# Four operations moved ahead of weight splits, and a tile by tile end, in a two-layer trunk on one core

## The reference, cut to what matters

```python
for l in range(2):
    x = x + 0.5 * swiglu(rmsnorm(x), ffn1_w_in[l], ffn1_w_out[l])       # hidden 2816
    z = rmsnorm(x) @ mix_w_in[l]                                         # 8 parts of 256 columns
    y_a = a_b * conv3(a_c * a_x)
    y_b = u * (tril(W_s) LN(v) + b)
    y_c = silu(LN(conv31(a * sigmoid(g))))
    y_d = scale * grouped_linear(avgpool(w) - w)
    x = x + concat(y_a, y_b, y_c, y_d) @ mix_w_out[l]
    x = x + cross_attention(rmsnorm(x), rmsnorm(mem), wq, wkv, wo)       # 4 heads of 256
    x = x + 0.5 * swiglu(rmsnorm(x), ffn2_w_in[l], ffn2_w_out[l])
return rmsnorm(x, norm_final)
```

## Time and profile before

| | |
|---|---|
| three runs | 1113.24, 1114.97, 1116.08 us (median 1114.97) |
| the profiled execution | 1115.91 us, of which 1113.0 us are the span from first to last instruction |
| PE busy | 1096.5 us (99% of the span), mean granted clock 0.996 |
| DVE, ACT, POOL busy | 710.8, 533.6, 396.1 us |
| read from HBM | 200.79 MB, 181 GB/s over the span |

### The profile page before, as it was taken

The page is one execution under the profiler, slowest core; times in us unless marked ns, Lnnn a source line. Parts: engine busy times, 40 slices in busy tenths (PEclk is TensorE's granted clock), DMA queues, the critical chain, the costliest instruction groups (busy, mean ns, idle before and its releaser), DMA issues.

```text
span 1113.0 us, 13974 instructions
## 1 busy us (share of the span) xinstructions
PE 1096.5 (99%) x5294; PEld 922.4 (83%) x5294; DVE 710.8 (64%) x821; ACT 533.6 (48%) x583; POOL 396.1 (36%) x775
## 2 busy tenths in 40 slices
PE   8999999999999999999999999999999999999996
PEld 6887888889798888888888888888988988888885
DVE  6666556799756656655566665568996557666552
ACT  5454434754545554444444544357454545444531
POOL 0677732000000056774226768210000002676700
PEclk9999999999999999999999999999999999999998
DMA  7977656553652477675766676556455436776651
GB/s 255 299 210 227 196 185 226 192 186 114 226 177 93 147 222 222 205 234 185 227 194 213 214 225 206 200 195 200 146 184 170 170 114 193 213 214 216 205 194 60
DMA packets 183330, 215.90 MB, mean 194 GB/s; under 512 B 18954, under 2 KB 138326, under 8 KB 183264
## 3 DMA queue, kind: packets, MB, share of 16 engines
q1 hardware_dynamic: 158112, 200.82, 55.4%
q0 software_dynamic: 24064, 13.16, 4.4%
q10 hardware_dynamic: 1088, 1.05, 0.3%
HBM read 200.79 MB, written 1.05 MB: 181 GB/s over the span
## 4 chain that ended last, share of the span: by engine, by line
PE 77%; DVE 9%; issue 6%; ACT 3%; POOL 2%; DMA 2%; DVEq 0%; SPq 0%; POOLq 0%; ACTq 0%
PE acc L1315 23%; PE acc L1317 23%; PE acc L1316 22%; DVE w_lo L747 4%; DVE arena L976 2%; POOL kT L409 2%; PE turn L1213 2%; PE acc L1332 1%; PE acc L1331 1%; PE acc L1333 1%; ACT w_hi L447 1%; PE acc L1482 1%; PE acc L1506 1%; DMA w_raw<-in_ffn_w_in 1%; DMA kT<-kT 1%
## 5 line engine op out<-in xcount | busy, mean ns | idle before, releaser
L747 DVE TENSOR_TENSOR w_lo<-w_raw,w_hi 128x2048 fp32r<-128x2048 f32 x191 | 428.1, 2247 | 228.9 <-ACT w_hi L447 228.6
L447 ACT CAST w_hi<-w_raw 128x2048 fp32r<-128x2048 f32 x191 | 357.1, 1871 | 152.3 <-PE acc L1317 132.2
L409 POOL DMA_DIRECT2D kT<-kT x704 | 345.8, 499 | 162.2 <-DVE kT L879 122.3
L1315 PE MATMUL acc<-w_hi,xT 128*128 128x512 f32 x808 | 316.7, 392 | 0.0
L1317 PE MATMUL acc<-w_hi,xT 128*128 128x512 f32 x808 | 314.7, 389 | 0.0
L1316 PE MATMUL acc<-w_lo,xT 128*128 128x512 f32 x808 | 314.4, 389 | 0.0
L1315 PE MATMUL acc<-w_hi,hT 128*128 128x512 f32 x544 | 214.7, 395 | 1.0 <-DVE hT L961 1.0
L1317 PE MATMUL acc<-w_hi,hT 128*128 128x512 f32 x544 | 212.0, 390 | 0.0
L1316 PE MATMUL acc<-w_lo,hT 128*128 128x512 f32 x544 | 211.7, 389 | 0.0
L398 POOL TENSOR_TENSOR rstd<-var,mhalf 128x2 f32<-128x2 f32 x14 | 24.2, 1730 | 488.7 <-DVE var L803 341.2
L1317 PEld LDWEIGHTS acc<-w_hi,xT 128*128 128x128 f32 x808 | 151.7, 188 | 32.0
(11 more groups left out here) (126 smaller groups left out, 860.8 us busy)
## 6 DMA issues: line engine op xcount, KB each, us to landing
w_raw<-in_ffn_w_in SPq DMA_DIRECT2D x174, 512.0 KB, 5.0
w_raw<-in_ffn_w_out SPq DMA_DIRECT2D x80, 512.0 KB, 4.4
w_raw<-in_mix_w_in SPq DMA_DIRECT2D x32, 512.0 KB, 4.5
w_raw<-in_xattn_wkv SPq DMA_DIRECT2D x32, 512.0 KB, 4.6
kT<-kT POOLq DMA_DIRECT2D x704, 16.0 KB, 3.3
w_raw<-in_mix_w_out SPq DMA_DIRECT2D x16, 512.0 KB, 4.1
w_raw<-in_xattn_wq SPq DMA_DIRECT2D x16, 512.0 KB, 4.5
w_raw<-in_xattn_wo SPq DMA_DIRECT2D x16, 512.0 KB, 4.5
```

The costliest lines, as they stand in the source:

```text
L409: pool.dma_start(hfeat[B * q:B * q + B, g % 2, a * RUN:(a + 1) * RUN], hblk[B * a:B * a + B, g % 2, q * RUN:(q + 1) * RUN]).then_inc(hfeat ...
L447: act.copy(w_hi[:, u % SLOTS, 0:n], w_raw[:, u % SLOTS, 0:n]).then_inc(w_split_hi, 1)
L747: dve.tensor_tensor(w_lo[:, u % SLOTS, 0:n], w_raw[:, u % SLOTS, 0:n], w_hi[:, u % SLOTS, 0:n].bitcast(F32), ALU.subtract).then_inc(w_spli ...
L1315: pe.matmul(o, hi, wh, start=(first and j == 0), stop=False)
```

## The change

Three edits change only the order of operations, once in each layer but the first. Memory rows are scaled after chunk 5 instead of chunk 6 (layer 0 only). The gate product L1002 goes ahead of DVE's split of U_MI+6. On ACT the silu and its high part go ahead of the split of U_MO+2; on DVE the low part of the silu goes ahead of every split that stood between L1099 and L961, those of U_MO+1 and U_MO+2.

The fourth edit is the end: PE takes the last two units row tile by row tile; each tile's half is updated, squared, meaned (one operation of 128x1, the share of the first half computed before), rooted and multiplied by itself; the first 512 columns get their gain before (`xg`) and their root from ACT, which also writes them out on its own queue; SP writes the other 512 columns. Each write is 256 KB. The gain row is loaded ahead of the last ffn's weights.

```diff
@@ SP
+                if l == L - 1:
+                    sp.wait_ge(mT_ready, L * 4)
+                    sp.dma_start(memT[:, 0:4, :]..., norm_final...).then_inc(gf_landed, 16)
                 ffn(l, U_F2I, v_f2i, v_f2o)
-            (the same two statements, here)
             for t in range(T):
                 sp.wait_ge(final_ready, t + 1)
-                sp.dma_start(out[0, t * P:(t + 1) * P, :], xs[:, t, :]).then_inc(out_landed, 16)
-            sp.wait_ge(out_landed, 16 * T)
+                sp.dma_start(out[0, t * P:(t + 1) * P, GN:D], xs[:, t, GN:D]).then_inc(out_landed, 16)
+            sp.wait_ge(out_landed, 16 * 2 * T)
@@ POOL
-                inv_sqrt(at.at(6, 8), V_X)
+                if l < L - 1:
+                    inv_sqrt(at.at(6, 8), V_X)
+            for t in range(T):
+                pool.wait_ge(var_ready, 2 + 6 * L + t)
+                pool.tensor_tensor(rstd[:, V_X, t:t + 1], var[:, V_X, t:t + 1], mhalf[:, t:t + 1], ALU.pow).then_inc(rstd_ready, 1)
@@ ACT
                 values(0)
-                weights_to(U_MO + 2, at)
...
-                squares(3, 1, at)
+                if l < L - 1:
+                    squares(3, 1, at)
+            for t in range(T):
+                act.wait_ge(x_updated, 16 * L + t + 1)
+                square(xs, 1, t, 8 + 16 * L - T + t)
+                act.wait_ge(xg_final, t + 1)
+                act.wait_ge(rstd_ready, 2 + 6 * L + t)
+                act.activation(xs[:, t, 0:GN], xg[:, t, :], ACT.Copy, scale=rstd[:, V_X, t:t + 1]).then_inc(left_ready, 1)
+                act.wait_ge(left_ready, t + 1)
+                act.dma_start(out[0, t * P:(t + 1) * P, 0:GN], xs[:, t, 0:GN]).then_inc(out_landed, 16)
@@ DVE
-                    if (l, f) == (0, 0) and c == 6:
+                    if (l, f) == (0, 0) and c == 5:
                         ...  # the memory rows' scaling, L888 to L890
                 mT_lo_part(3)
-                weights_to(U_MI + 6, at)
                 for t in range(T):
                     ...  # the gate product, L1001 to L1003
+                weights_to(U_MI + 6, at)
...
-                weights_to(U_MO + 2, at)
                 y_lo(3, 4, y32)
                 weights_to(U_MO + 3, at)
...  # last layer only, in place of update, update, variance(V_X), and L1201 over 1024 columns
+            for t in range(T):
+                dve.tensor_tensor(xg[:, t, :], xs[:, t, 0:GN], gf[:, 0:GN], ALU.mult).then_inc(xg_final, 1)
+            dve.wait_ge(x_squared, 8 + 16 * L - T)
+            dve.tensor_scalar(var[:, V_PART, :], sumsq[:, 0, :], 1.0 / D, EPS, ALU.mult, ALU.add).then_inc(part_ready, 1)
+            dve.wait_ge(part_ready, 1)
+            for t in range(T):
+                update(3, 1, t, U_F2O + 10 + t, F2O_PAIR[1], 0.5, last, tiles_done=T)
+                dve.wait_ge(x_squared, 8 + 16 * L - T + t + 1)
+                dve.scalar_tensor_tensor(out=var[:, V_X, t:t + 1], in0=sumsq[:, 1, t:t + 1], scalar=1.0 / D,
+                                         in1=var[:, V_PART, t:t + 1], op0=ALU.mult, op1=ALU.add).then_inc(var_ready, 1)
+                dve.wait_ge(rstd_ready, 2 + 6 * L + t)
+                dve.scalar_tensor_tensor(out=xs[:, t, GN:D], in0=xs[:, t, GN:D], scalar=rstd[:, V_X, t:t + 1],
+                                         in1=gf[:, GN:D], op0=ALU.mult, op1=ALU.mult).then_inc(final_ready, 1)
@@ PE
+                        if (l, f, n) == (L - 1, 1, 1) and j >= NGO - 2:
+                            continue
...
+            def last_units():
+                for t in range(T):
+                    for j in (NGO - 2, NGO - 1):
+                        unit(U_F2O + NGO + j, Layer(L - 1), F2O_PAIR[1], hT_hi, hT_lo, GK * j, False, j == NGO - 1, tiles=[t])
```

More of the change, by code:

```diff
@@ L144, in trunk_kernel @@
         qscale = sb("qscale", [P, T])
-        V_MEM, V_X, V_MIX, V_SGU, V_CLN, V_Q, V_F2 = range(7)
+        V_MEM, V_X, V_MIX, V_SGU, V_CLN, V_Q, V_F2, V_PART = range(8)
         def cut(at, *shape):
@@ L226, in trunk_kernel @@
         passed = sem("passed")
-        final_ready, out_landed = sem("final_ready"), sem("out_landed")
+        xg_final, part_ready = sem("xg_final"), sem("part_ready")
+        left_ready, final_ready, out_landed = sem("left_ready"), sem("final_ready"), sem("out_landed")
         NBLK, RUN, SHUFFLES = P // B, 2 * T * B, 16
@@ L361, in _ @@
                             unit(u, at, wide_parts(u, src, l, GK * j, GK, col + n * GN))
+                if l == L - 1:
+                    sp.wait_ge(mT_ready, L * 4)
+                    sp.dma_start(memT[:, 0:4, :].rearrange("p k s -> p (k s)"),
+                                 norm_final.rearrange("(o d) -> o d", o=1).to_broadcast([P, D])).then_inc(gf_landed, 16)
                 ffn(l, U_F2I, v_f2i, v_f2o)
-            sp.wait_ge(mT_ready, L * 4)
-            sp.dma_start(memT[:, 0:4, :].rearrange("p k s -> p (k s)"),
-                         norm_final.rearrange("(o d) -> o d", o=1).to_broadcast([P, D])).then_inc(gf_landed, 16)
             for t in range(T):
                 sp.wait_ge(final_ready, t + 1)
-                sp.dma_start(out[0, t * P:(t + 1) * P, :], xs[:, t, :]).then_inc(out_landed, 16)
-            sp.wait_ge(out_landed, 16 * T)
+                sp.dma_start(out[0, t * P:(t + 1) * P, GN:D], xs[:, t, GN:D]).then_inc(out_landed, 16)
+            sp.wait_ge(out_landed, 16 * 2 * T)
         @block.gpsimd
@@ L851, in extra, with update @@
                     dve.tensor_copy(sguT[:, i, :, :].rearrange("p h t -> p (h t)"), tb[1][:, :]).then_inc(sguT_ready, 1)
-            def update(b, n, t, u, pair, factor, at):
-                dve.wait_ge(unit_done, at.at(2 * UNITS, 2 * SLOTS + 2 * u + t + 1))
+            def update(b, n, t, u, pair, factor, at, tiles_done=None):
+                dve.wait_ge(unit_done, at.at(2 * UNITS, 2 * SLOTS + 2 * u + (tiles_done or t + 1)))
                 cols = xs[:, t, n * GN:(n + 1) * GN]
@@ L1188, in _ @@
                     xT_lo_part(4, 0, 1, at)
[L1189 to L1197, removed]
+                weights_to(UNITS - 1, at)
+                if l < L - 1:
+                    weights_to(UNITS, at)
+                    update(3, 1, 0, U_F2O + 11, F2O_PAIR[1], 0.5, at)
+                    weights_to(UNITS + 1, at)
+                    update(3, 1, 1, U_F2O + 11, F2O_PAIR[1], 0.5, at)
+                    dve.wait_ge(x_squared, at.at(16, 8 + 16))
+                    variance(V_X, steps)
+            gf = memT[:, 0:4, :].rearrange("p k s -> p (k s)")
             dve.wait_ge(gf_landed, 16)
-            gf = memT[:, 0:4, :].rearrange("p k s -> p (k s)")
+            dve.wait_ge(x_updated, 16 * L)
             for t in range(T):
-                dve.scalar_tensor_tensor(out=xs[:, t, :], in0=xs[:, t, :], scalar=rstd[:, V_X, t:t + 1], in1=gf,
+                dve.tensor_tensor(xg[:, t, :], xs[:, t, 0:GN], gf[:, 0:GN], ALU.mult).then_inc(xg_final, 1)
+            dve.wait_ge(x_squared, 8 + 16 * L - T)
+            dve.tensor_scalar(var[:, V_PART, :], sumsq[:, 0, :], 1.0 / D, EPS, ALU.mult, ALU.add).then_inc(part_ready, 1)
+            dve.wait_ge(part_ready, 1)
+            last = Layer(L - 1)
+            for t in range(T):
+                update(3, 1, t, U_F2O + 10 + t, F2O_PAIR[1], 0.5, last, tiles_done=T)
+                dve.wait_ge(x_squared, 8 + 16 * L - T + t + 1)
+                dve.scalar_tensor_tensor(out=var[:, V_X, t:t + 1], in0=sumsq[:, 1, t:t + 1], scalar=1.0 / D, in1=var[:, V_PART, t:t + 1],
+                                         op0=ALU.mult, op1=ALU.add).then_inc(var_ready, 1)
+                dve.wait_ge(rstd_ready, 2 + 6 * L + t)
+                dve.scalar_tensor_tensor(out=xs[:, t, GN:D], in0=xs[:, t, GN:D], scalar=rstd[:, V_X, t:t + 1], in1=gf[:, GN:D],
                                          op0=ALU.mult, op1=ALU.mult).then_inc(final_ready, 1)
@@ L1298, in first_unit, with unit @@
                     ins.then_inc(unit_done, 1)
-            def unit(u, at, pair, s_hi, s_lo, k0, first, last, before=None, between=None):
+            def unit(u, at, pair, s_hi, s_lo, k0, first, last, before=None, between=None, tiles=range(T)):
                 pe.wait_ge(w_split, at.at(UNITS, SLOTS + u + 1))
@@ L1305, in unit @@
                 nk = unit_kt(u)
-                for t in range(T):
+                for t in tiles:
                     if before:
@@ L1533, in _ @@
                 ffn(l, U_F2I, 1, lambda t: None if t else x_turn(3, 1, 1, "f2in11", at))
+            last_units()
 _INS = ["x", "mem", "norm_ffn1", "ffn1_w_in", "ffn1_w_out", "norm_mix", "mix_w_in", "sconv_w", "sgu_norm_g", "sgu_w", "sgu_b",
```

## The result

The changed kernel is slightly slower: 1116.07 us (median of 22 runs, 1112.37 to 1118.19) against 1113.91 for the kernel before (22 runs, 1112.12 to 1116.08), ratio 1.0017 with a 95% interval of 1.0011 to 1.0023. That is +1.9 us where -1.5 was forecast: inside the range, but on the other side, and clear of the measurement's interval. The profiled execution took 1115.74 us with a span of 1113.4.

What follows compares the result with a forecast made beforehand. PE, busy 1096.5 of 1113.0 us, was taken as the bound. Terms -1.1 -1.2 +2.9 -2.1 sum to -1.5, taking the median 1114.97 to 1113.5; own range 1111.5 to 1115.5, 8-in-10 range 1110.4 to 1116.8.

Steps and rivals of the forecast that it cites:

- Memory rows, -1.1: Layer 0, scaling moved one chunk earlier: PE's wait for the memory rows goes, gaining 1.1 us (bounds 0.9 and 1.1).
- gate products, -1.2: Once per layer, gate product ahead of DVE's split: PE's wait goes, 1.2 us gained for both layers, restart included.
- The cover named for the scaling: After chunk 5, DVE's 1.31 us idle before the next split absorbs the 1.4 scaling: cost nothing, 0.1 if short.
- The conversion of a wait into time lost: On PE, a wait costs its idle time plus 0.16 us of lost overlap between products.
- Silu, +1.43 per layer: PE's silu wait becomes a wait for U_MO+1's split, queued behind the low part: 1.43 us more per layer, +2.9 in all.
- the second rival: PE's two stalls of about 2.0 us drop the clock to half rate: +3.0 in all, time 1116.5, chance 0.09.
- The end, -2.1: After the last products, tile-by-tile order, half-tile operations and smaller writes save 2.1 us (bounds -1.5 and -3.3).
- Gain row, 0: Its 512 KB load ahead of the last ffn's loads on SP costs nothing; without cover, 4.5 us at most.
- the silu edit gains: Rival: both silu waits of PE go, -1.6 us, sum -6.0, time 1109.0; chance 0.13.
- the end gives little: Rival: ACT's writes land late or small operations wait for each other; end -0.4, time 1115.2, chance 0.12.

## Why the prediction was wrong, point by point

Two terms of the sum failed: the end, taken at -2.1, and the fall of the clock behind the waits for weights, taken at nothing.

- **Memory rows, -1.1, and gate products, -1.2: right where PE waits.** Together -2.3 measured. The traces have 0.6 for each gate product. For the memory rows they have 1.1, but of the four profiled kernels that scale them late only two wait for them at all. The term came from one execution and was taken for all; its mean is not known and is smaller. The cover named for the scaling was there: DVE's idle time before the next split shrank from 1.31 to 0.24. (The prediction's working has a slip of 0.1 here: 1.41 of scaling does not fit into 1.31, and 94.3 and 1.02 make 95.3.) The conversion of a wait into time lost (idle time plus the 0.16 of overlap) held.
- **Silu, +1.43 per layer: the mechanism was right, and so was the price of the wait itself** (1.46 in layer 1 of the changed kernel). The two waits have the forecast length and releaser, the low part came when it should, DVE idled 3.55. **What failed is the clock behind the waits, which stood in the sum at nothing:** the silu edit measured +4.8 and not +2.9, because of what stands under the second rival, "the clock falls in the stall". It was given 0.09 on the ground that 2.0 lies between 0.9, which did nothing, and 2.7, which did, each read from one execution. But the wait of 2.2 to 3.0 at the kernel's start has the clock fall behind it in 7 of the 11 traces that show it. In the profiled executions with waits of 2.0 the clock fell behind 4 of 6: one of two in the changed kernel, two of two with the silu edit alone, one of two with the roots moved. So it was neither the rival's "both" nor the forecast's "neither" but about one fall, 1.6, in the mean. A middle value should have been in the sum, as half of 2 x 1.5; -1.5 would have become 0.
- **The end, -2.1: wrong by 1.4 or 1.5, and here it was the path that failed.** The chain of operations was right (3.1 from update to issue; the writes took 2.5 from SP's queue and 2.7 from ACT's, and the later one counts). But its result was taken to be the end of the kernel. The row of what SP waited for at the close stood in the profile of before too, and so did GpSimd's drain, tied with the landing to 0.03 us. What was late next after the shortened chain was not asked. -0.7 was measured (0.56 between the traces), and -2.0 with the roots elsewhere (2.5 between the traces).
- **Gain row, 0: right.** No run moved it alone, but the last ffn, whose loads stand behind it, takes PE 227.93 in both kernels. A high split waits for its load once more than before (three times, 6.8 in all); these waits are at 15.4, 30.5 and 36.1, far from the gain row.
- **Rivals.** That the silu edit gains (1109.0) was rightly held improbable; something near it, 1109.95, was measured only with the split put back. That the end gives little happened, by a mechanism that the text did not name. Two of the rivals were thus true together, one of them by half, and their sum (+1.6 +1.5 on -1.5) makes +1.6 where +1.9 was measured. Each had been given its chance as if it came alone. That the result still lies inside the stated range is luck: the range was drawn wide enough for a fall in both layers, and the kernel before measured 1.1 lower here than the 1114.97 from which the forecast was counted.

The Trainium skill's formula for a write (DMA: Bandwidth & Descriptors, Anatomy of one DMA) would, as an estimate and for a DMA issued by GpSimd, have made 256 KB 0.6 quicker than 512 KB. Here the landing went from 2.7 to 2.5 on the same queue and took 2.7 on ACT's, so the row was the better guide. The clock fell to 0.50 behind idle time and rose again under work, in the traces named above. The Trainium skill's rule that idle time throttles the array (TensorE: Matmul & The Clock Gate, Part 1) agrees with that.

## What to carry to other kernels

When an operation is moved ahead of a deferred batch of work, write down every item of the batch that now stands behind it: here it was two splits and not one, and the nearer one was what PE needed next. A stall of TensorE is priced twice, by its length and by the chance of a fall of the clock behind it; here the fall, when it came, cost 1.6 and the longer wait 1.4 or 1.5. A wait that one profile shows can be absent in the next execution, so read two or three before it goes into a sum at full size. Before shortening the last chain of a kernel, look at what else the closing barrier waits for; here an engine's drain was tied with the landing already.

## What the runs showed of the hardware that was not expected

- GpSimd's closing drain took 5.9 to 6.1 us from its last small operation (128x1 or 128x2) in all nine traces where it had one near the end. What makes it that long was not tested. With no work for it there, nothing waited for it. DVE's drain took 0.8 to 2.5 over the same stretch, mostly its own last operation.
- The clock fell after idle times of 2.0 in one layer and not in the other of the same execution (4 of 6 in three traces). It did not after 1.0 (0 of 2), and did after 4.4 (2 of 2), each time to 0.50 for 3.4 us or twice that. Behind a wait of 2.0 it shows 0.3 to 1.1 after the restart: in the changed kernel the first six products after the wait still start 0.23 to 0.30 apart.
- The same step is in the start of the kernel before: in its profiled execution the clock was 0.50 from 18.1 to 21.5, in that of the changed kernel it was 1.00 there. That alone makes two profiled spans differ by nearly as much as the change did, so the spans of one pair of profiles (1113.0 and 1113.4) could not have told what the change costs.
